# A one-layer encoder step on one core: modulation rows, sums of squares and the last tiles rearranged

## The reference

```python
mod = silu(c) @ w_ada + b_ada            # (1024) @ (1024, 6144)
sh1, sc1, g1, sh2, sc2, g2 = split(mod, 6)
h = rmsnorm(x, norm1) * (1 + sc1) + sh1
xa, ga, us = split(h @ w_in, 3)          # 512 columns each
y_lru = rglru(causal_conv(xa)) * gelu(ga)
gy = gelu(s5_scan(us))
y_s5 = gy * sigmoid(gy @ s5_w_glu + s5_b_glu)
x = x + g1 * (concat(rmsnorm(y_lru, gn_lru), rmsnorm(y_s5, gn_s5)) @ w_out)
h = rmsnorm(x, norm2) * (1 + sc2) + sh2
x = x + g2 * peer(h)                     # 8 heads, top 16 of 128 x 128 experts
y = rmsnorm(x, norm_f)
```

## Time and profile before

| | us |
|---|---|
| median of 3 runs (range) | 3261.43 (3260.09 to 3261.61) |
| profiled execution, its own time | 3262.26 |
| its span, first to last instruction | 3260.4 |
| PE busy in the span | 3010.9 (92%) |
| DVE busy | 2513.9 (77%) |
| POOL busy | 1500.4 (46%) |
| ACT busy | 802.6 (25%) |

### The profile page before, as it was taken

How to read it: one execution, slowest core, us unless ns; L and a number is a source line. 1 busy time by engine, 2 the same in 40 slices (tenths; PEclk the granted TensorE clock), 3 DMA queues, 4 the chain that set the end, 5 groups by cost and what they waited for, 6 DMA issues and landing times.

```text
span 3260.4 us, 47647 instructions
## 1 busy us (share of the span) xinstructions
PE 3010.9 (92%) x16232; PEld 2446.8 (75%) x16232; DVE 2513.9 (77%) x5687; ACT 802.6 (25%) x1584; POOL 1500.4 (46%) x1211
## 2 busy tenths in 40 slices
PE   8999789979999657759999999999999999999996
PEld 8566566456666447758888888888888888888885
DVE  6381303437878899879999999999999999999997
ACT  3114111034444469811111111111111111111112
POOL 0000000003556500057677667676667776677661
PEclk9989897989999979979999999999999999999998
DMA  5012641068888627799999999999999999999995
GB/s 199 7 51 47 158 144 55 0 260 332 332 334 331 231 72 200 204 366 402 392 392 389 393 390 393 391 395 392 386 395 394 391 388 396 392 394 390 386 397 212
DMA packets 360076, 959.45 MB, mean 294 GB/s; under 512 B 37376, under 2 KB 152112, under 8 KB 349952
## 3 DMA queue, kind: packets, MB, share of 16 engines
q0 software_dynamic: 147456, 536.94, 42.1%
q1 hardware_dynamic: 199968, 416.78, 35.4%
q10 hardware_dynamic: 12544, 4.47, 0.7%
HBM read 841.10 MB, written 116.85 MB: 294 GB/s over the span
## 4 chain that ended last, share of the span: by engine, by line
PE 84%; ACT 5%; DVE 4%; DMA 4%; issue 2%; POOL 0%; ACTq 0%; DVEq 0%; SPq 0%
PE ps L900 30%; PE ps L889 24%; PE ps L777 7%; PE ps L756 4%; PE ps L673 4%; PE ps L800 3%; DMA arena<-in_w_ada 2%; PE ps L623 2%; PE ps L596 2%; ACT arena L1169 2%; ACT u_turn L1103 2%; ACT arena L1186 1%; PE ps L863 1%; PE ps L789 1%; PE ps L707 1%
## 5 line engine op out<-in xcount | busy, mean ns | idle before, releaser
L900 PE MATMUL ps<-w,v_rows 128*128 128x320 f32 (+1 forms) x4096 | 1033.9, 406 | 0.9 <-DVE y_sum L1259 0.9
L900 PEld LDWEIGHTS ps<-w,v_rows 128*128 128x128 f32 x4096 | 763.7, 190 | 203.7 <-DVE y_sum L1259 1.4
L554 POOL DMA_INDIRECT ring<-in_vt,arena x512 | 701.0, 1369 | 282.2 <-DVE y_rows L1752 187.8
L554 POOL DMA_INDIRECT ring<-u_table,arena x512 | 559.5, 1093 | 467.1 <-DVE ring L1738 218.6
L889 PE MATMUL ps<-h_hi,u_hi 128*128 128x320 f32 (+1 forms) x2048 | 654.6, 320 | 36.3 <-DVE u_lo L1259 34.7
L1752 DVE SCALAR_TENSOR_TENSOR y_rows<-ring,s5c,y_rows 128x1024 f32<-128x1024 f32 x512 | 652.4, 1274 | 11.8 <-DMA ring<-in_vt,arena 11.8
L1738 DVE SCALAR_TENSOR_TENSOR ring<-ring,h_rows 128x1024 f32<-128x1024 f32 x512 | 623.3, 1218 | 11.9 <-DMA ring<-u_table,arena 5.1
L889 PE MATMUL ps<-h_hi,u_lo 128*128 128x320 f32 (+1 forms) x2048 | 608.2, 297 | 0.0
L889 PE MATMUL ps<-h_lo,u_hi 128*128 128x320 f32 (+1 forms) x2048 | 608.2, 297 | 0.0
L889 PEld LDWEIGHTS ps<-h_hi,u_hi 128*128 128x128 f32 x2048 | 390.6, 191 | 43.4 <-DVE u_lo L1259 35.4
L1208 ACT ACTIVATE w<-ps 128x320 f32<-128x320 f32 (+1 forms) x256 | 104.7, 410 | 1253.4 <-PE ps L889 1236.9
(11 more groups left out here) (234 smaller groups left out, 3159.9 us busy)
## 6 DMA issues: line engine op xcount, KB each, us to landing
u_turn<-in_ut SPq DMA_DIRECT2D x128, 512.0 KB, 6.8
u_table<-u_turn SPq DMA_DIRECT2D x128, 512.0 KB, 6.2
u_raw<-in_ut SPq DMA_DIRECT2D x128, 512.0 KB, 6.8
v_rows<-in_vt SPq DMA_DIRECT2D x64, 1024.0 KB, 8.8
coef_dram<-arena SPq DMA_DIRECT2D x9, 4096.0 KB, 16.4
c_raw<-coef_dram SPq DMA_DIRECT2D x64, 576.0 KB, 8.9
arena<-in_w_ada SPq DMA_DIRECT2D x32, 512.0 KB, 5.2
arena<-in_w_ada SPq DMA_DIRECT2D x4, 2048.0 KB, 12.7
```

The costliest lines, as they stand in the source:

```text
L554: nc.gpsimd.indirect_dma_start(out=slot(n), out_offset=None, in_=table, in_offset=bass.IndirectOffsetOnAxis(ap=uvi[:, at:at + 1], axis=0)) ...
L900: last = mm(ps[4 + m % 4][:, 0:width], seg(v_in_buf, 2048 * r + 1024 * e + P * d, P), seg(w_in_buf, ow, width), start=n == 0, stop=n == 3)
```

## The change

The first modulation is now computed as the second is: the conditioning is the weight, 512 columns of `w_ada` move, four products' worth of rows are copied by ACT (`mod_row`) and turned to columns by 16 small products (stage `modA`). `x` is loaded right after the first chunk of `w_ada`, and the third and fourth chunk wait until `x` has landed. The second modulation moves in 16 chunks of 256 columns, 1024 KB each; the first is loaded early, the second and third only when the last `y` product is done, since two of the buffers now lie where the S5 states stood.

The sums of squares: DVE adds the four squared channel tiles of a half into one (`summed`), so 9 products a half are left; ACT squares y_lru ahead of the glu jobs and y_s5 one channel tile at a time, DVE multiplies y_s5 a tile at a time. The sums of y_lru run on PE ahead of the last glu tile, those of y_s5 after it.

The end: `g2` and `norm_f` are loaded two score banks earlier; `x1` comes in a part for tiles 0 to 2 and the rest. DVE does sparse tiles 0 to 2 after additions 3, 5 and 7, the eight last row additions after additions 8 to 15, and scales tiles 0 to 2 after additions 13 to 15, with a square root of their own on ACT. The fourth sparse tile and the dense tiles follow as before.

Places in the arena:

```diff
-WGLU, MODB = 22272, (35360, 36384, 24320)
-MROW, GYT, YS5, SQ = 38400, 26112, 34848, (9216, 13568)
+WGLU, MODB = 22272, (35360, 4416, 6464)
+MROW, MROW0, GYT, YS5, SQ = 38400, 17920, 26112, 34848, (9216, 13568)
```

SP, first loads:

```diff
             for n in range(4):
+                if n == 1:
+                    sp.wait_ge(s("w_ada_in0"), 16)
+                    load(ar(X0, 8192).rearrange("p (k d) -> p k d", k=8), A["xp"], "x_in")
+                    load(ar(X0 + 8192, 1024, DSEQ), A["xs"], "x_in")
+                if n == 2:
+                    sp.wait_ge(s("x_in"), 32)
                 load(ar(WADA[n], 4096).rearrange("p (k n) -> p k n", k=8), wv[:, :, 512 * n:512 * n + 512],
                      f"w_ada_in{n}")
-                if n == 1:
-                    sp.wait_ge(s("w_ada_in0"), 16)
-                if n == 3:
-                    sp.wait_ge(s("w_ada_in1"), 16)
...
```

SP, loads of the second modulation:

```diff
             def load_mod(n):
-                load(ar(MODB[n % 3], 1024).rearrange("p (k n) -> p k n", k=8),
-                     wv[:, :, 2048 + P * n:2048 + P * n + P], f"w_ada_in{n % 3}")
+                load(ar(MODB[n % 3], 2048).rearrange("p (k n) -> p k n", k=8),
+                     wv[:, :, 2048 + 256 * n:2048 + 256 * n + 256], f"w_ada_in{n % 3}")
...
             load_mod(0)
-            load_mod(1)
...
-            load_mod(2)
...
-            for n in range(3, NMOD):
-                if n % 4 == 2:
-                    sp.wait_ge(bank_full, where["modB", n // 4 - 1] + 1)
+            sp.wait_ge(bank_full, where["y", 11] + 1)
+            sp.wait_ge(s("fin_ready"), 1)
+            load_mod(1)
+            load_mod(2)
+            for n in range(3, NMOD // 2):
+                if n % 2 == 0:
+                    sp.wait_ge(bank_full, where["modB", (n - 3) // 2] + 1)
                 else:
-                    sp.wait_ge(s("mod_done"), n - 2 - (n - 2) // 4)
+                    sp.wait_ge(s("mod_done"), (n - 3) // 2 + 1)
                 load_mod(n)
...
-            sp.wait_ge(s("ys5_ready"), 1)
+            sp.wait_ge(s("ys5_ready"), ML)
             load(ar(X1, 8192).rearrange("p (k d) -> p k d", k=8), A["xp"], "x_again_in")
```

SP, last loads:

```diff
+            sp.wait_ge(s("s_bank_full"), 4 * 64 - 2)
+            load(seg(g2_buf, 0, 1024), g2d, "g2_back")
+            load(seg(norm_f_buf, 0, 1024), A["norm_f"], "norm_f_in")
             sp.wait_ge(s("s_bank_full"), 4 * 64)
-            load(seg(g2_buf, 0, 1024), g2d, "g2_back")
-            load(seg(x1_buf, 0, 8192), x1d[:, 0:8192], "x1_back")
...
+            load(seg(x1_buf, 0, 3072), x1d[:, 0:3072], "x1_back")
+            load(seg(x1_buf, 3072, 5120), x1d[:, 3072:8192], "v_in0")
```

PE, first modulation:

```diff
-            b = bank_for(pe, "mod", 0)
             for n in range(4):
+                b = bank_for(pe, "mod", n)
                 pe.wait_ge(s(f"w_ada_in{n}"), 16)
                 w = ar(WADA[n], 4096).rearrange("p (k n) -> p k n", k=8)
-                for j in range(4):
-                    for k in range(8):
-                        last = mm(b[:, 8 * n + 2 * j:8 * n + 2 * j + 2], w[:, k, P * j:P * j + P], cs[:, k, :],
-                                  start=k == 0, stop=k == 7)
-            full(last)
+                for k in range(8):
+                    last = mm(b[0:2, :], cs[:, k, :], w[:, k, :], start=k == 0, stop=k == 7)
+                full(last)
+
+            def rows_to_columns(stage, rows_of, at, n_cols):
+                stage_emptied(pe, rows_of)
+                b = bank_for(pe, stage, 0)
+                for n in range(n_cols):
+                    last = mm(b[:, 2 * n:2 * n + 2], ar(at + P * n, P, 2), ident[0:2, 0:2], start=True, stop=True)
+                full(last)
+
+            rows_to_columns("modA", "mod", MROW0, 16)
```

PE, second modulation: 16 chunks, two to a bank:

```diff
-                    last = mm(b[0:2, P * (n % 4):P * (n % 4) + P], cs[:, k, :], w[:, k, :], start=k == 0, stop=k == 7)
+                    last = mm(b[0:2, 256 * half:256 * half + 256], cs[:, k, :], w[:, k, :], start=k == 0, stop=k == 7)
```

PE, sums of squares:

```diff
+            def token_sums(half):
+                for t in range(NTILE):
+                    c0, n = cols(t)
+                    last = mm(ps[where["rms", 0] % 8][0:n, 9 * half + t:9 * half + t + 1], ar(SQ[half] + c0, n),
+                              ones[:, :], start=True, stop=True)
+                return last
+
             for m in range(ML):
+                if m == ML - 1:
+                    bank_for(pe, "rms", 0)
+                    pe.wait_ge(s("sums_ready"), 1)
+                    token_sums(0)
...
-                    for k in range(4):
-                        last = mm(b[0:n, 9 * half + t:9 * half + t + 1], ar(SQ[half] + NT * k + c0, n),
-                                  ones[:, :], start=k == 0, stop=k == 3)
-            full(last)
+            pe.wait_ge(s("sums_ready"), 2)
+            full(token_sums(1))
```

DVE, around the glu products:

```diff
+            dve.wait_ge(s("sq_ready"), 1)
+            for m in range(1, ML):
+                summed(0, m)
+            for m in range(ML):
+                last = scaled(YL, "gnl", m)
...
-            stage_emptied(dve, "glu")
-            tt(ar(YS5, 4352), ar(YS5, 4352), ar(GYT, 4352), ALU.mult).then_inc(s("ys5_ready"), 1)
...
+            for m in range(ML + 1):
+                if m < ML:
+                    stage_emptied(dve, "glu", 3 * m + 3)
+                    y = ar(YS5 + NT * m, NT)
+                    tt(y, y, ar(GYT + NT * m, NT), ALU.mult).then_inc(s("ys5_ready"), 1)
+                if m:
+                    dve.wait_ge(s("sq_ready"), m + 1)
+                    if m > 1:
+                        summed(1, m - 1)
+                    last = scaled(YS5, "gns", m - 1)
```

DVE, last 16 additions:

```diff
             for m in range(16):
                 add_up(31, m)
-                if m % 2 == 0:
-                    add_row(63, 1, m // 2)
...
+                if m in (3, 5, 7):
+                    sparse_sum((m - 3) // 2)
+                if m >= 8:
+                    add_row(63, 1, m - 8)
...
+                if m == 13:
+                    dve.wait_ge(s("roots_ready"), 7)
+                    link(V.reciprocal(rms4[:, 20:23], rms4[:, 20:23]))
+                    dve.wait_ge(s("norm_f_in"), 16)
+                if m >= 13:
+                    scaled_out(m - 13)
```

More of the change, by code:

```diff
@@ L711, in _ @@
                     full(last)
-            stage_emptied(pe, "modB")
-            b = bank_for(pe, "modT", 0)
-            for n in range(NMOD):
-                last = mm(b[:, 2 * n:2 * n + 2], ar(MROW + P * n, P, 2), ident[0:2, 0:2], start=True, stop=True)
-            full(last)
+            rows_to_columns("modT", "modB", MROW, NMOD)
             stage_emptied(pe, "modT")
```

124 lines of the change are left out of this document (77 added, 47 removed).

## The result

| | before | after |
|---|---|---|
| median, us (range) | 3261.52 (3260.09 to 3267.85) | 3203.02 (3202.10 to 3203.54) |
| profiled execution, us | 3262.26 | 3203.0 |
| span, us | 3260.4 | 3201.2 |
| mean granted clock | 0.963 | 0.968 |

Four runs of each; the ratio is 0.9816, 95% interval 0.9804 to 0.9827: 1.8% faster. The forecast was 3203.

A forecast was written before the change was run, and what follows sets the result against it. The prediction put 84% of the span on TensorE, so stages shorten only if its work shrinks or starts sooner. Its terms, -7 - 21 - 22 - 8 = -58, took 3262.3 to 3204, median 3203 us; range 3190 to 3220 for 8 in 10.

The forecast's parts named there:

- First modulation, -7: Front: 64 products of 512 columns replace 256 instructions; transposes start at 59.5 instead of 66.5 us; bounds -11 and +11.
- Second modulation, -21: Second modulation, from 351.45 us: chunks of 3.5 us of products, DMA-bound, ending at 421 instead of 442; bounds -31 and +3.
- the sum of packet times: Second modulation: 15360 packets of 1 KB take 45 us, S5 store and reload 23.8, together 69 us of queue time.
- Sums, -22: Sums of squares around glu: 18 products among the glu jobs, 18 after; mix starts at 501 to 502 instead of 523.8.
- The end, -8: After the last V product: three sparse tiles and scalings moved earlier; scaling ends at 3248.6 instead of 3256.7; bounds -10, -3.
- the walk: DVE under the last V products, step by step: sparse tiles end at 3204.6, 3208.5 and 3212.4; PE does not wait.
- the sum: Whole kernel: -7 - 21 - 22 - 8 = -58, so 3262.3 becomes 3204 and the median 3203.
- the range: Whole kernel: measured time between 3190 and 3220 us, for 8 in 10.
- The first (PE sets the pace at once): Second modulation: packet times overlap, so PE sets the pace at once; -31 there, 3193 in all; chance 0.11.
- The second (wider rows buy nothing): Second modulation: bytes stay at the old 167 GB/s, stage ends near 442, -37 is left, 3224; chance 0.07.
- The third: The end: sparse tiles wait for `x1`, DVE 4.6 us late, the end gains only 3.5, 3207; chance 0.07.
- The fourth: Both modulations: PE stays at 1.2 GHz, second-modulation chunks take 6.9 us; slower by 8, 3270; chance 0.05.

The follow-up runs named there:

- the part alone: The kernel before with only the new sums of squares (18 products instead of 72, work spread over glu): 3231.36 us, ratio 0.9904.
- the second modulation alone: The kernel before with only the second modulation in 16 chunks of 256 columns: 3245.78 us, ratio 0.9951.
- the three parts that keep the old sums: The kernel before with one part each: first modulation as rows 3255.45 us, second modulation in 256-column chunks 3245.78 us, sparse tiles under the last V products 3251.94 us.

## Why the prediction was right

- **First modulation, -7.** The mechanism was as told: 9.61 us for the cold first chunk, 23.24 for the other three together (forecast 9 and twice 6.9), small products 5.56 (5.3), DVE ready at 53.35 (53.5). Two sizes were off in the compared profiles. The second chunk landed at 32.99 and not at 31, so the products ended at 56.2 and not 54, and the transposes started at 62.39 and not 59.5. From 12.3 us to that landing the engines had moved some 7.4 MB, 0.8 more than the tokens and this chunk hold: the next chunks, issued from 27.8 us on when the tokens had landed, took their share, which at 387 GB/s is an estimated 2 us. And one more group of transposes ran at the slow pace. But -3.2 is one pair of profiles: with the new rows the input projection started at 75.84, 74.25, 72.14, 75.35 and 71.83 us, with the old at 79.07, 78.93, 80.30, 79.64 and 80.00, so on average 5.7 us earlier. The start at 72.14 had the small products in 3.73 us, one group of transposes at 1.97 and one at 1.53; the start at 75.84 had 5.56 and three at 1.97: the same instructions at the two clocks.
- **Second modulation, -21.** Forecast DMA-bound to 421, in fact DMA-bound to 389 and then paced by PE. By its start at 346.77 the stage took 72.7 us where 69.5 were forecast. It is made up otherwise than the sum of packet times that gave 69.5: 61.0 us of products (forecast 56; 3.6 to 3.7 a chunk, but 4.27 in the four from 370 us on, at a granted clock of 0.82), the five waits of 11.06, and 0.67 for the last copy. So the near hit in size is partly luck. The reason given for the waits, S5 traffic and w_ada on the same engines, is shown by the runs that moved the traffic. Against the old stage's other profiles (84.7 to 91.3 us) the gain is 12 to 19.
- **Sums, -22.** -22.7 in the pair and in the part alone. The products behind the last tile cost 3.88 us (forecast 3.7). Two other terms were off by 1 us each and cancelled: the products ahead of the last glu tile cost 1.98 and not 3, and from the last sigmoid to the mix it took 8.41 (469.35 to 477.76) and not 7.4, as the scaling that the forecast took to be hidden stands between the two additions.
- **The end, -8.** In before's time (51.4 us later) the sparse tiles ended 0.9 us behind the walk, the scaling at 3249.1 (3248.6 forecast); 1.1 came from the 64 steps, where the 0.87 us wait for `y_added` is gone, and 7.8 behind them. From ACT's last read of the squares to the first scaling it is 1.03 us now and 2.05 before, 1.02 less with the table load gone from there. By the Trainium skill (ScalarE: Activation LUTs, "What ACT_TABLE_LOAD costs") a switch costs 2.66, and so much would have gone. The trace shows no drain beside the 1.28 us load: before, the load starts 0.01 us behind the last read and the first root 0.02 us behind the load.
- **What was not in the sum.** -4.8 in the coefficient blocks and +1.0 ahead of the V products, which no term named: 15 idle waits alone bring both, in the one execution of that kernel, so they are luck and no part of the mechanism. -1.5 ahead of the second modulation is the clock: that stretch took 270.9 to 271.0 us in seven of the profiles and 272.2 to 272.5 in six, with and without the new front. From 76.5 to 95 and from 95 to 106 us behind the start of the projection the granted clock was 0.62 to 0.64 and 0.83 to 0.86 in the seven, 0.60 to 0.61 and 0.72 to 0.75 in the six, and the 128 products of 137 columns there take 9.2 to 9.7 us against 10.1 to 10.5. What decides between the two is not shown. Without these three the time would have been about 3208. The shortfalls in the two modulations and the unforeseen gain happen to cancel; that the median fell on 3203 to the microsecond is luck, that it lies in the range is not.
- **Rivals.** The first (PE sets the pace at once) is refuted by the five waits, though from 389 us on it is what happens. The second (wider rows buy nothing) is refuted by the second modulation alone: 72.05 us. The rule beside it, the Trainium skill (DMA: Bandwidth & Descriptors, "Specifications"), line rate from 512 bytes on, is not borne out either: with the engines full, 512-byte pieces move 291 GB/s (the row below) and the 2 KB rows of the first modulation 387, though the former are a store and not a load. The loads agree if one divides by the busy share, an estimate since packet times overlap: 220/0.77 = 286 GB/s for 512 bytes, 243/0.74 = 328 for the 1 KB rows beside no S5 traffic. By this estimate wider rows bought bandwidth as well as fewer waits; how much of the gain is which, no run here separates. The third is refuted by the first sparse tile, which waits for nothing. The fourth is refuted by 3.61 us a chunk at a clock of 0.92 and 0.95.

The store of the coefficient blocks in the kernel before, in 512-byte pieces with nothing else of size beside it, in the view by windows:

```profile
1223.00:1228.00 5.00, 4.07 (x32) 3.72 (x32) 5.00 (x17) 4.97 (x13) 0.00 (x0) 1.00 1.02 291
```

## What to carry to other kernels

Count the instructions on the path before moving them: 54 fewer one-column products gave 19 of the 23 us, the better place of the rest 3. The waits for a load that came from other traffic on the same DMA engines moved with that traffic inside the stage, and went only when it left the stage: look for a stage that does not read through the same engines. And before a few microseconds in an untouched loop are credited to an edit, shift that loop's code by a few idle instructions and measure again.

## What the runs showed of the hardware

- A loop on DVE took 199 us or 4.8 less, and 15 idle waits ahead of it were enough to change it, with 17 or 18 packets of about 8 KB on an instruction queue in the long case (the kernel before, and the three parts that keep the old sums) and 6 to 8 in the short one. Behind DVE's stops of 2.5 to 3.2 us PE was granted a lower clock (0.62 from 1263 to 1271 us). The Trainium skill (Runtime: NRT & Kernel Launch, "Instruction fetch mechanics") says that a taken branch to a page outside the current window makes the engine fetch it by DMA first; the packets beside the stops agree with it.
- With the DMA engines full (shares 1.02 and 1.05) a store in 512-byte pieces moved 291 GB/s and a load in 2 KB rows 387.
- The one execution profiled can lie at the end of a stage's own spread: the unchanged second modulation took 84.7 to 91.3 us, the unchanged front of the changed kernel 71.8 to 75.8.
